# The double norm ahead of the last block: product with the learnt row on GpSimd, tile by tile

## What is computed

```python
def first_block(...):
    ...
    return rms_norm(x, final_g)

def second_block(x, ln1, w_in, ...):
    ...
        h = rmsnorm(x, ln1[l])
        proj = h @ w_in[l]
```

## Time and profile before

| what | us |
|---|---|
| median of 3 runs | 2902.42 (2898.55 to 2903.85) |
| the profiled execution, its own time | 2891.92 |
| its span from first to last instruction | 2890.1 |
| TensorE busy | 2605.7 (90%) |
| VectorE busy | 1306.7 (45%) |
| ScalarE busy | 1003.4 (35%) |
| GpSimd busy | 349.1 (12%) |
| mean granted clock of TensorE | 0.956 of full speed |

### The profile page before, as it was taken

The page is one execution under the profiler, slowest core; times in us unless marked ns, Lnnn a source line. Parts: engine busy times, 40 slices in busy tenths (PEclk is TensorE's granted clock), DMA queues, the critical chain, the costliest instruction groups (busy, mean ns, idle before and its releaser), DMA issues.

```text
span 2890.1 us, 35654 instructions
## 1 busy us (share of the span) xinstructions
PE 2605.7 (90%) x14064; PEld 1531.7 (53%) x14064; DVE 1306.7 (45%) x2537; ACT 1003.4 (35%) x1857; POOL 349.1 (12%) x188
## 2 busy tenths in 40 slices
PE   5999996899999997796869999998699997999998
PEld 3885575333333322674644333332477786787886
DVE  2496545234444444477442333332655554443342
ACT  4216542343434343425522222221344333322222
POOL 0210020001111101220100000000123320121221
PEclk9999998799999998899989999999899997999999
DMA  7117732699999998220029999999221002222321
GB/s 246 60 58 263 253 111 102 244 326 351 358 366 347 357 361 303 76 85 1 30 77 387 387 386 386 387 386 377 71 74 44 12 16 77 90 93 88 102 80 51
DMA packets 303261, 568.52 MB, mean 197 GB/s; under 512 B 12656, under 2 KB 55792, under 8 KB 302968
## 3 DMA queue, kind: packets, MB, share of 16 engines
q1 hardware_dynamic: 294480, 545.33, 53.1%
q0 software_dynamic: 3840, 12.59, 1.9%
q10 hardware_dynamic: 4776, 8.33, 0.9%
HBM read 551.53 MB, written 14.68 MB: 196 GB/s over the span
## 4 chain that ended last, share of the span: by engine, by line
PE 41%; DMA 5%; DVE 4%; ACT 1%; issue 1%; POOL 0%; DVEq 0%; ACTq 0%; SPq 0%
PE PS L969 8%; PE PS L1072 4%; PE PS L1071 4%; PE PS L1070 4%; PE PS L1083 3%; PE PS L1084 3%; PE PS L1085 3%; PE PS L1023 2%; DMA WIDE<-in_w_gate_dram 2%; PE PS L1060 2%; DMA RING<-in_w_gate_dram 1%; PE PS L751 1%; PE PS L1187 1%; PE PS L1192 1%; PE PS L1115 1%
## 5 line engine op out<-in xcount | busy, mean ns | idle before, releaser
L2558 POOL TENSOR_TENSOR WHL<-RING,WHL 128x1024 fp32r<-128x1024 f32 x64 | 171.1, 2674 | 1606.8 <-ACT WHL L1303 1606.8
L969 PE MATMUL PS<-RING,RF 128*64 128x512 f32 x1448 | 351.6, 612 | 13.0 <-DMA RING<-in_w_gate_dram 3.9
L969 PE MATMUL PS<-WIDE,RF 128*64 128x512 f32 x1408 | 331.9, 601 | 9.7 <-DMA WIDE<-in_w_gate_dram 3.5
L1303 ACT ACTIVATE WHL<-RING 128x1024 fp32r<-128x1024 f32 x129 | 134.5, 1048 | 233.3 <-PE PS L1085 146.2
L969 PEld LDWEIGHTS PS<-RING,RF 128*64 128x64 f32 x1448 | 92.6, 138 | 221.3 <-issue 200.6
L1070 PE MATMUL PS<-RR,WHL 128*128 128x512 f32 x512 | 203.8, 398 | 1.1 <-DVE RR L2311 1.1
L1072 PE MATMUL PS<-RR,WHL 128*128 128x512 f32 x512 | 204.1, 399 | 0.0
L1071 PE MATMUL PS<-RR,WHL 128*128 128x512 f32 x512 | 201.8, 394 | 0.0
L969 PEld LDWEIGHTS PS<-WIDE,RF 128*64 128x64 f32 x1408 | 92.6, 136 | 203.9 <-issue 182.6
L1547 ACT ACTIVATE RF<-PS,MODS,MSC 128x128 f32<-128x128 f32 x192 | 77.2, 437 | 302.9 <-PE PS L1023 156.4
L1799 DVE TENSOR_TENSOR WHL<-RING,WHL 128x1024 fp32r<-128x1024 f32 x65 | 80.7, 1242 | 203.6 <-ACT WHL L1303 203.6
(11 more groups left out here) (383 smaller groups left out, 4895.4 us busy)
## 6 DMA issues: line engine op xcount, KB each, us to landing
RING<-in_w_gate_dram SPq DMA_DIRECT2D x83, 1024.0 KB
WIDE<-in_w_down_dram SPq DMA_DIRECT2D x74, 1024.0 KB, 9.8
RING<-in_w_up_dram SPq DMA_DIRECT2D x70, 1024.0 KB
WIDE<-in_w_up_dram SPq DMA_DIRECT2D x57, 1024.0 KB, 11.6
RING<-in_w_down_dram SPq DMA_DIRECT2D x51, 1024.0 KB
RING<-in_ada_w_dram SPq DMA_DIRECT2D x48, 1024.0 KB
WIDE<-in_w_gate_dram SPq DMA_DIRECT2D x45, 1024.0 KB, 11.3
RING<-in_w_in_dram SPq DMA_DIRECT2D x30, 1024.0 KB
```

What stands on the lines that cost most here:

```text
L969: ins = e.matmul(a[r:r + 64, :], xs[:, j, 0:64], w[:, i, :], start=j < 2, stop=j > 5)
L1303: e.activation(h, load_buffer(ld)[:, js, cs], ACT.Copy).then_inc(act, A(("hi", st["i"])))
L2558: e.tensor_tensor(lo, load_buffer(loads[st["load"]])[:, js, cs], h.bitcast(F32), ALU.subtract).then_inc(pool, G(("lo", st["i"])))
```

## The change

The product moves from VectorE's loop to GpSimd, behind the walk through the experts' plan, and its signal from the counter V to G. The wait for FG moves with it. The squares of X now write their elements into HN2, and the squares of XG into a buffer for each tile. The waits of GpSimd are, as VectorE's were, on the second addition of each tile.

```diff
--- before.py
+++ after.py
@@ -648,7 +648,7 @@
 
 
         HTH2, HTL2 = rr(0, 8, 512), rr(4096, 8, 512)
-        XG, HN2, JUNK = ar(0, 4, 1024), ar(4096, 4, 1024), [ar(8192, 1024), ar(9216, 1024)]
+        XG, HN2, JUNK = ar(0, 4, 1024), ar(4096, 4, 1024), [ar(8192 + 1024 * t, 1024) for t in range(4)]
         KTOK, VTOK = ar(0, 4, 4, 128), ar(2048, 4, 4, 128)
         C = ar(4096, 12, 512)
         Z = ar(10240, 4, 512)
@@ -1738,9 +1738,9 @@
 
             for t in range(4):
                 e.wait_ge(dve, V["sent", 1, 7, t, 1])
-                square(JUNK[0], "2a", t, X, 0)
-                e.wait_ge(dve, V["xg", t])
-                square(JUNK[1], "2b", t, XG, 16)
+                square(HN2[:, t, :], "2a", t, X, 0)
+                e.wait_ge(pool, G["xg", t])
+                square(JUNK[t], "2b", t, XG, 16)
                 root("2a", t, 6)
                 if t:
                     root("2b", t - 1, 20)
@@ -2479,11 +2479,8 @@
                 e.wait_ge(dve, V.n)
                 e.tensor_scalar(HN2[:, t, :], XG[:, t, :], rr_, None, ALU.mult).then_inc(dve, V(("hn", "2b", t)))
 
-            e.wait_ge(rows_in, 16)
             for t in range(4):
                 r, r2 = SM[:, 6 + t:7 + t], SM[:, 20 + t:21 + t]
-                e.wait_ge(dve, V["sent", 1, 7, t, 1])
-                e.tensor_tensor(XG[:, t, :], X[:, t, :], FG, ALU.mult).then_inc(dve, V(("xg", t)))
                 mean_square("2a", t)
                 if t:
                     norm_scale(t - 1)
@@ -2598,6 +2595,10 @@
                                              None, compute_op=ALU.add).then_inc(added, 16)
                         e.indirect_dma_start(XROWS, bass.IndirectOffsetOnAxis(SLOT[0:32, n + 4:n + 5], 0), YC[ex % 2],
                                              None, compute_op=ALU.add).then_inc(added, 16)
+            e.wait_ge(rows_in, 16)
+            for t in range(4):
+                e.wait_ge(dve, V["sent", 1, 7, t, 1])
+                e.tensor_tensor(XG[:, t, :], X[:, t, :], FG, ALU.mult).then_inc(pool, G(("xg", t)))
             weights(12 + 1)
             cau = CON[:, C_CAU:C_CAU + 128].unsqueeze(1).to_broadcast([128, 4, 128])
```

## The result

| | before | after |
|---|---|---|
| median of 8 runs, same chip | 2899.17 us (2896.08 to 2903.85) | 2890.45 us (2883.39 to 2893.47) |
| ratio of after to before | | 0.9967 [0.9958, 0.9977] |
| the profiled execution, its own time | 2891.92 | 2889.08 |
| its span | 2890.1 | 2887.3 |
| TensorE busy | 2605.7 | 2615.7 |

The changed kernel is faster by 9.6 us by the ratio (0.0033 x 2899, interval 6.7 to 12.2); the two medians stand 8.7 apart. GpSimd has the four products more, VectorE less. TensorE shows 10.0 us more busy time for the same matmuls, at a lower mean clock. Most of that, 8.1 us, lies ahead of the last addition (1829.4 against 1821.3), where TensorE's work is the same; 2.5 us lie behind the projection's first matmul, and those are what the prediction didn't have.

The account below looks back on a forecast made before the run. The prediction took a ladder between VectorE and ScalarE to bound the stretch before the projection; an earlier start, shorter tile steps and one blocked scaling summed to a gain of 8.6 us, off 2902.42: 2893.8 us, range 2890.0 to 2899.0.

Parts of the forecast that it names:

- what follows has no clock of its own: From the second block's projection on, TensorE only waits on earlier instructions, so the ladder's whole gain reaches the end.
- B: Rival: projection starts at the low clock, up to 4.2 us lost, 2898.0 us; taken as 0; chance 0.14.
- C: Rival: gain given back further on by clock drops, a late load or late GpSimd products; 2898 to 2903; chance 0.12.
- The base: Time the gain was taken off: 2902.42 us, the median of the runs shown.
- Products still running: VectorE's first scaling blocked by GpSimd's fourth product, ending about 0.4 us late, once.
- Start of the ladder: First root behind the last addition: at 2043.0 in place of 2046.52, gain 3.5 us.
- ScalarE's step: In the ladder, with products ready, each tile takes ScalarE 2.30 us, which sets the step by a hair.
- Last turning: TensorE's turning of the last tile: 11.7 us behind the last addition's start in place of 20.3.
- Junk buffers: A buffer per tile and squares into HN2 let the early square leave the additions' operands alone; cost 0.
- The table load: ScalarE's 1.28 us load for the root follows tile 0's second square, ends before 2042, hidden under the additions.
- A: Rival: VectorE's small statistics wait for GpSimd's products too; gain 5.0 to 7.4, 2895.0 to 2897.4 us; chance 0.12.
- D: Rival: VectorE and GpSimd hold each other up; loses above 5.2 us per product, 2915 at 8.4; chance 0.04.

Follow-up runs that it names:

- e1: Kernel before with only the junk buffers changed, the product staying on VectorE; ratio to before 0.9996.
- e2: Changed kernel with all four GpSimd products waiting for the last addition; ratio to before 0.9997.
- e5b_warm: Changed kernel plus 26 unread identity transposes on TensorE between the experts' last matmul and the turning of the tiles; ratio to before 0.9978.
- e0_after_again: Changed kernel measured again without an edit; 2893.22 against 2900.16 us, ratio to before 0.9978.
- e6b_ladder_early: Changed kernel with tile 0's statistics and tile 1's first mean between VectorE's last additions, junk buffers at other offsets; ratio to before 0.9980.
- e4b_products_twice: Changed kernel with each GpSimd product made twice in the same place; ratio to before 1.0011.
- e3_vector_between: Changed kernel with the products back on VectorE, each right behind its tile's additions, none on GpSimd; ratio to before 0.9977.
- f3: Repeat of e7b: changed kernel with early statistics and early table load; 2890.86 against 2900.22 us, ratio to before 0.9967.
- e7b: e6b_ladder_early plus a root of a constant ahead of ScalarE's first square, loading the table early; median 2890.13 us, ratio to before 0.9973.
- f4: e7b's edits plus 10 identity transposes on TensorE ahead of the turning; 2885.76 against 2900.22 us, ratio to before 0.9955.
- the two warm traces: Traces of e5b_warm and its repeat, the changed kernel with 26 identity transposes; ratios to before 0.9978 and 0.9965.
- the early-table one: The kernel of e7b and f3, changed kernel with early statistics and early table load; ratios to before 0.9973 and 0.9967.

## Why the prediction came out as it did

The direction and the rough size held: a gain of 8.6 forecast, and 9.6, 6.4 and 9.6 by the ratios of three measurements (8.7, 6.9 and 9.0 by the medians). The time itself was further off than the gain: 2893.8 forecast and 2890.45 measured, 0.45 above the lower end of the range, with three of the eight executions below it. Three steps were off: one of mechanism, two of size.

**The step that failed: "what it gives back reaches the end only if what follows has no clock of its own. I take it that it has none", and with it the zeros of B and C.** TensorE's granted clock is such a clock. Three traces of three of the changed kernel lose 1.0 at the projection's start and 1.5 to 1.6 in the stretch of the scores against the kernel before: 2.4 to 2.9 of the 9.1 are given back. The 1.0 is the projection's first 2.3 us at 0.50; the 1.6 is the low stretch at the start of the scores, some 87 to 91 us behind the projection's first matmul, in all three traces of the changed kernel and in none of the kernel before, e1 or e2. Rival B was right in kind, at a quarter of its bound of 4.2. That was to be read from the earlier trace rows: the clock had risen there just before the projection, and a projection that comes closer behind the first turning could meet it still low. "The rise comes with the work" was a choice, and it counted the work only roughly. C was right in kind with its "other clock drops". I put each loss into a rival and took both at 0, where a term of 0 to 4 with a middle of 2 was due; the forecast from the last addition on would then have been 6.6, and the traces' net is 6.5. That 2 is seen only from the result. The medians can't decide between 6.5 and 8.6: their intervals are 6.7 to 12.2, 3.8 to 9.3 and 5.8 to 13.3 us. That two of them have 9.6 in the middle is no proof that nothing was given back, since the traces show it. So far as the total came near 8.6 although 2.6 had been left out, that is luck, or something ahead of the ladder that no run isolates.

**The base was mis-sized.** The gain was taken off 2902.42, the median of three runs; the median of eight is 2899.17. These 3.25 are nearly the whole 3.35 between forecast and measured time. With 2899.17 the same sum gives 2890.6, and that this meets the measured 2890.45 to 0.1 is luck too, as intervals of 5 us and more say.

Where B drew on "TensorE: Matmul & The Clock Gate" of the Trainium skill (PE-mode transpose: transposes don't bring the full clock; its figures there are for bf16), these runs speak against the rule for fp32 transposes. In e5b_warm only transposes stand between the experts' last matmul and the projection; the clock fell among them and rose again among them, and the projection starts at the full level. In e2_behind_last eight transposes took 1.97, the low level, and after 16 more the projection's matmuls were 0.23 apart from the first on: the clock had risen over transposes alone.

**A term of the sum that was mis-sized: "Products still running", 0.4, measured 0 to 0.08.** The products took 2.35 each, not 2.4, and the last addition itself started 6.33 behind T0 in place of 6.08, so they ended at 2049.82, 3.91 behind its start (forecast 2046.5 - 2042.2 = 4.3); the first scaling ended 0.57 behind their end by its own time. In e0_after_again it took 0.83 and ended 0.55 behind. The block is real (2.02 in e2_behind_last, 2.27 in e6b_ladder_early), and the changed kernel misses it by a hair; that is luck. With it off, the pairs of roots stand 2.27 apart and the ladder gains 9.1, inside my 7.9 to 9.3.

**The steps that held.** Start of the ladder: the first root 0.78 behind the last addition's start, forecast 0.80. ScalarE's step: 2.27, forecast 2.30. Last turning: 11.2, forecast 11.7. GpSimd's product at 2.35 and additions undisturbed. Junk buffers at 0, by e1_junk_only; what they were said to be for is not borne out by the code (see there). The table load hidden under its activation's wait. The one instruction behind the products on GpSimd had 22.35 us of idleness left, forecast 30.

**The rivals.** A is out: the small instructions took 0.14 to 0.28 inside the products. D didn't occur; its break-even of 5.2 per product fits e4b_products_twice, where 4.9 each left 1.2. That the engines do hold each other up, a little, is seen there too. But the rival had no price for the clock, and with it the change would have lost already at 4.9. "Engine selection" of "GPSIMD Engine Reference" in the Trainium skill advised against the move: e3_vector_between is the version that follows it. It loses 2.4 us in its trace against the changed kernel and nothing in the median.

**What stays open.** Why the clock falls more often in the stretch of the scores in some traces. The low stretch at its start is there in the three traces of the changed kernel, in e4b, e6b and f3, and not in before, e1, e2, e3, e7b, f4 or the two warm traces. It doesn't hang on the clock at the projection's start: f3 began the projection at the full level and has it. The blocks ahead of it are equal to 0.1 (18.80 in both), and the stretch takes 134.6, 136.1 to 136.6, 137.6 to 137.7, 139.1 or 140.7, as if in steps of 1.5, without an order in how early the projection starts. In the traces it repeats from run to run for before's neighbours (e1, e2), the changed kernel and the warm one, and not for the early-table one. Whether the median run of each kernel is the same as its profiled one there was not seen, and for the warm kernel it isn't.

## What to carry to other kernels

Where a pass runs tile after tile between two engines and its first step needs no more than its tile, queue that step ahead of the work it waited behind without need, or on an idle engine even at half the speed: here the order was worth 6.5 of 8.9 us and the engine the rest. On GpSimd it is best over before VectorE's first wide operation from SBUF to SBUF (here 2.02 and 2.27 in place of 0.75 where it wasn't). And price TensorE's clock as a term, not as a rival: an earlier start behind a quiet stretch can begin at the low level, and drops further on can change with it, here 2.6 of 9.1 us. Judge such edits stretch by stretch from a common point, since single traces differ by up to 11 us ahead of it, and take the base of a forecast from more than three runs.

## What the runs showed of the hardware that was not expected

- The granted clock rose while TensorE did nothing but fp32 transposes (e2_behind_last, e5b_warm, e7b_ladder_table, and before the change). 26 transposes of the identity put its fall off: 1.06 and 1.09 us for the next two times eight in place of 1.29 and 1.97, and then 3 us at 0.50.
- VectorE's 128x1 instructions, with two pointer scalars too, are not held by GpSimd; a 128x1024 tensor-scalar from SBUF is (0.75 grew to 2.02 and 2.27). It ended 0.55 behind the end of the product that was running, in both cases and in e0_after_again, e4b_products_twice and e7b_ladder_table (0.83, 1.00, and 1.26 for the second). GpSimd's next product then took longer in its turn (2.67 in place of 2.34): they alternate, and the price is set by how much of the running product is left.
- A kernel whose critical ladder was 1.2 us shorter in its trace measured 3 us slower (1.0011 [1.0001, 1.0021]).
